# One encoder layer with a mixture of experts: the slot table's twelve scatters and its load go into GpSimd's overflow branch

## The reference, cut to what matters

```python
def _hier_moe(h, w_rg, b_rg, w_re, b_re, w_gate, w_up, w_down):
    ...
    grp_1h = jax.nn.one_hot(jnp.argmax(g_logits, -1), N_GROUPS, dtype=jnp.float32)
    ...
    top_v, top_i = lax.top_k(e_logits, TOP_K)
    top_w = jax.nn.softmax(top_v, axis=-1) * p_grp
    ...
    for e in range(N_EXPERTS):
        he = jax.nn.silu(t @ w_gate[e]) * (t @ w_up[e])
        y = y + comb[:, e:e + 1] * (he @ w_down[e])
```

## Time and profile before

| | |
|---|---|
| median of 3 runs | 1020.76 us (1020.22 to 1023.59) |
| profiled execution, span | 1024.1 us |
| TensorE busy | 910.2 us (89%) |
| GpSimd busy | 317.1 us (31%) |
| VectorE, ScalarE busy | 528.9 and 231.9 us |
| DMA moved | 165.11 MB, mean 161 GB/s |
| mean granted TensorE clock | 0.953 of 2.4 GHz |

### The profile page before, as it was taken

The page is one execution under the profiler, slowest core; times in us unless marked ns, Lnnn a source line. Parts: engine busy times, 40 slices in busy tenths (PEclk is TensorE's granted clock), DMA queues, the critical chain, the costliest instruction groups (busy, mean ns, idle before and its releaser), DMA issues.

```text
span 1024.1 us, 10105 instructions
## 1 busy us (share of the span) xinstructions
PE 910.2 (89%) x3322; PEld 470.7 (46%) x3322; DVE 528.9 (52%) x830; ACT 231.9 (23%) x578; POOL 317.1 (31%) x352
## 2 busy tenths in 40 slices
PE   4999999999979999999999999948969999999800
PEld 4555466444534444445567445544434444444300
DVE  4999999964533298736236554363311111111156
ACT  5321423333572112000014202131101111111101
POOL 6920043333454333300014313122342211122146
PEclk9999999999999999999999999967989999999955
DMA  9310300420020003120050314175998999998462
GB/s 340 137 42 0 124 0 22 143 61 22 1 95 30 1 0 122 43 83 1 0 205 1 121 44 164 62 307 224 417 378 318 417 422 418 389 413 346 165 256 116
DMA packets 46197, 165.11 MB, mean 161 GB/s; under 512 B 8640, under 2 KB 14144, under 8 KB 33856
## 3 DMA queue, kind: packets, MB, share of 16 engines
q1 hardware_dynamic: 39424, 151.85, 38.3%
q0 software_dynamic: 6720, 12.60, 3.3%
HBM read 156.88 MB, written 18.03 MB: 171 GB/s over the span
## 4 chain that ended last, share of the span: by engine, by line
PE 84%; POOL 4%; DVE 3%; ACT 3%; issue 3%; DMA 2%; POOLq 0%; DVEq 0%; ACTq 0%
PE ps L2009 17%; PE ps L2475 8%; PE ps L2504 7%; PE ps L2306 7%; PE ps L2171 6%; PE ps L2478 5%; PE ps L2241 5%; PE ps L2345 5%; PE ps L2279 5%; PE ps L2187 3%; PE ps L2137 2%; PE ps L2452 2%; PE ps L2112 2%; PE ps L2160 2%; PE ps L2148 2%
## 5 line engine op out<-in xcount | busy, mean ns | idle before, releaser
L1327 DVE SCALAR_TENSOR_TENSOR cat<-early,cpar,cat 128x798 f32<-128x798 f32 (+2 forms) x150 | 143.7, 958 | 4.9
L846 POOL TENSOR_SCALAR hT<-hT,rinv 128x512 f32<-128x512 f32 (+1 forms) x48 | 67.9, 1426 | 93.2 <-DVE rinv L1449 93.2
L2009 PE MATMUL ps<-ring,hT 128*128 128x512 f32 (+1 forms) x256 | 91.7, 519 | 0.0
L2009 PE MATMUL ps<-hT,ring 128*128 128x256 f32 (+1 forms) x256 | 84.7, 493 | 4.1 <-issue 2.5
L912 POOL DMA_INDIRECT pair_rows<-hT,sidx x22 | 22.1, 1005 | 182.0 <-DVE hT L1936 181.1
L1926 DVE COPY memx<-ps 128x256 f32<-128x256 f32 x22 | 9.3, 424 | 131.2 <-PE ps L2487 131.2
L2009 PEld LDWEIGHTS ps<-ring,hT 128*128 128x128 f32 x256 | 48.9, 193 | 39.6 <-issue 37.2
L2009 PEld LDWEIGHTS ps<-hT,ring 128*128 128x128 f32 x256 | 49.5, 194 | 38.0 <-issue 32.5
L853 POOL TENSOR_SCALAR memx<-memx,rinv 128x256 f32<-128x256 f32 x24 | 22.1, 927 | 129.6 <-DVE rinv L1405 129.6
L720 POOL TENSOR_SCALAR lnt<-mv 128x1 f32<-128x1 f32 x28 | 14.2, 508 | 154.6 <-DVE mv L748 153.4
L2504 PE MATMUL ps<-ring,memx 128*64 128x512 f32 (+1 forms) x144 | 58.8, 602 | 0.7 <-DVE memx L1926 0.7
(11 more groups left out here) (337 smaller groups left out, 1748.4 us busy)
## 6 DMA issues: line engine op xcount, KB each, us to landing
ring<-w_down SPq DMA_DIRECT2D x16, 1024.0 KB, 16.6
early<-w_gate SPq DMA_DIRECT2D x12, 1024.0 KB, 9.4
early<-w_up SPq DMA_DIRECT2D x12, 1024.0 KB, 13.4
ring<-w_gate SPq DMA_DIRECT2D x10, 1024.0 KB, 12.4
ring<-w_up SPq DMA_DIRECT2D x10, 1024.0 KB, 16.0
scr<-w_down SPq DMA_DIRECT2D x8, 1024.0 KB, 15.4
cat<-w_down SPq DMA_DIRECT2D x8, 1024.0 KB, 15.3
scr<-w_gate SPq DMA_DIRECT2D x5, 1024.0 KB, 9.2
```

The lines of the kernel that those rows point to most:

```text
L846: g.tensor_scalar(sprob[u % 4][:, 0:width], sprob[u % 4][:, 0:width], rinv[:, u % 4:u % 4 + 1], None, ALU.mult).then_inc(prob_ready, 1)
L1327: ins = v.scalar_tensor_tensor(out=out, in0=src, scalar=cpar[:, c, k:k + 1], in1=out, op0=ALU.mult, op1=ALU.add)
L2009: last = t.matmul(out_of(bank), lhs(k), rhs(k), start=(k == 0), stop=(k == KC - 1))
```

## The change

The twelve table scatters leave the loop of m = 2 and go to the start of GpSimd's branch for `n_over > 0`. The table's load leaves SyncE and is issued by GpSimd in the same branch, behind the wait for the scatters; the wait for the load stands there too. If `n_over` is zero, none of this is run. Nothing else differs.

```diff
--- before.py
+++ after.py
@@ -668,9 +668,6 @@
                     load_d(n % D_SLOTS, expert(n))
             sp.wait_ge(ctl_ready, 1)
             load_gb(3)
-            sp.wait_ge(table_done, 16 * 2 * NT)
-            sp.dma_start(tab[:, 0:BLOCKS * NE * 2].rearrange("p (b c) -> p b c", b=BLOCKS),
-                         table_dram.rearrange("(b p e) t -> p b (e t)", p=P, b=BLOCKS)).then_inc(tab_in, 16)
             n_over = sp.value_load(ctl[0:1, 0:1], min_val=0, max_val=LIST)
             with sp.Fori(0, LIST // 2) as i:
                 with sp.If(2 * i < n_over):
@@ -948,21 +945,23 @@
                     gather(m + 2)
                 if m >= 1:
                     scatter(m - 1)
-                if m == 2:
-                    pool.wait_ge(table_init, 16)
-                    for k in range(2):
-                        pool.wait_ge(slots_ready, k + 1)
-                        for i in range(NT):
-                            g.indirect_dma_start(table_dram, bass.IndirectOffsetOnAxis(ap=slots[:, k, i:i + 1], axis=0),
-                                                 tvals[:, i, k, :], None, bounds_check=T * NE - 1,
-                                                 oob_is_err=False).then_inc(table_done, 16)
             scatter(NSB - 1)
             pool.wait_ge(ctl_ready, 1)
-            pool.wait_ge(tab_in, 16)
             for b in range(2):
                 pool.wait_ge(rows_out[b], 16 * (NSB // 2))
             n_over = pool.value_load(ctl[0:1, 0:1], min_val=0, max_val=LIST)
             with pool.If(n_over > 0):
+                pool.wait_ge(table_init, 16)
+                for k in range(2):
+                    pool.wait_ge(slots_ready, k + 1)
+                    for i in range(NT):
+                        g.indirect_dma_start(table_dram, bass.IndirectOffsetOnAxis(ap=slots[:, k, i:i + 1], axis=0),
+                                             tvals[:, i, k, :], None, bounds_check=T * NE - 1,
+                                             oob_is_err=False).then_inc(table_done, 16)
+                pool.wait_ge(table_done, 16 * 2 * NT)
+                g.dma_start(tab[:, 0:BLOCKS * NE * 2].rearrange("p (b c) -> p b c", b=BLOCKS),
+                            table_dram.rearrange("(b p e) t -> p b (e t)", p=P, b=BLOCKS)).then_inc(tab_in, 16)
+                pool.wait_ge(tab_in, 16)
                 with pool.Fori(0, LIST // 2) as i:
                     with pool.If(2 * i < n_over):
                         cs = [pool.value_load(ctl[0:1, bass.ds(1 + LIST + 2 * i + b, 1)], min_val=0,
```

## The result

The changed kernel takes 1017.5 us in the median of 20 runs (1015.57 to 1024.77), the kernel before 1023.29 in 20 runs (1019.61 to 1029.38). The ratio is 0.9948 with a 95% interval of 0.9931 to 0.9966: faster by 5.3 us, 3.5 to 7.1. I had forecast 7.9 and, from the 3 runs then known, 1012.9 with a range up to 1017.0. So the direction was right, and the time is 0.5 us outside the range.

The account below looks back on a forecast made before the run. TensorE and the weight stream were taken as two near limits. Landing 7.5 + 0.4 = 7.9 us earlier at down(11), end 0: span 1024.1 to 1016.2, less 3.3 for the runs' median, 1012.9 us; range 1009.0 to 1017.0.

Parts of the forecast that it names:

- The burst holds gather(5) up: On GpSimd, twelve table scatters take 15.6 us before gather(5); without them it issues near 736.5 and TensorE's 8.33 us wait goes.
- TensorE's lead: How much earlier TensorE runs after down(3): 10.05 us gained less 1.5 us of waiting, 8.5 us (7.0 to 9.5).
- the wait at down(3): TensorE waits 0.5 to 3.0 us, taken as 1.5, for weights delayed by row transfers that move ahead.
- The weights set the start of down(11): At down(11) the weight load's landing, 7.9 us earlier (7.0 to 8.6), decides the start, not TensorE.
- the filled gap: The half-empty weight stream from 764 to 778 us fills, moving the landing for down(11) forward by 7.5 us.
- the first rival: The weight stream keeps some 3 us of its gap or loses speed to earlier row transfers: gain 5, 1015.8 us; 10%.
- The wait grows from 1.8 to some 2.2, and the gain from there is 7.9 us: At down(11) TensorE arrives at 847.7 and the weights at 849.9, so the kernel gains 7.9 us.
- the sign that I gave: Sign of being right: TensorE waits 1 to 4 us for weights at down(11).
- the stall at T(5): TensorE's 8.33 us wait for gather(5) before T(5), plus 1.7 us of work behind it at the 1.2 GHz clock.
- After down(11) nothing is given back: After down(11) every load waits on a buffer TensorE frees, so both move together and the gain stays.
- The end costs nothing: After the last scatter, the removed table load frees no time and the branch over a longer body costs 0 us.
- the jump: Rival: the branch over the longer overflow body costs an instruction fetch, 0 to 4.3 us, middle 2.2, giving 1015.1; 9%.

Follow-up runs that it names:

- b_spread: The kernel before, with the twelve table scatters issued one per turn, m = 2 to 13, instead of all in m = 2: ratio to before 0.9971, stage 260.1 us.
- a_warm18: The changed kernel with 18 unused 128x128 products on TensorE ahead of down(11): ratio to the kernel before 0.9928, stage 257.3 us.
- b_swap2: The kernel before with gate and up loads of experts 21 and 30 moved behind down matrices of 17, 18 and 26, 27: ratio 0.9996, stage 263.4 us.
- a_swap2: The changed kernel with gate and up loads of experts 21 and 30 moved behind down matrices of 17, 18 and 26, 27: 1012.65 us, ratio to before 0.9902.
- a_warm: The changed kernel with 36 unused 128x128 products on TensorE ahead of down(11): ratio to the kernel before 0.9972, stage 260.9 us.

## Why the prediction was right or wrong, point by point

- **The burst holds gather(5) up**: right. gather(5) was forecast at 736.5; it is at 737.42 in a trace whose stage starts 0.86 later. T(5) waits for nothing. b_spread shows that it is the burst.
- **TensorE's lead**: forecast 8.5 (7.0 to 9.5), measured 9.5, as T(6) to gu(10) all start 8.62 us earlier in a stage that starts 0.86 later. I had put the wait at down(3) at 1.5 us, and it is 0.36.
- **The weights set the start of down(11)**: right as a mechanism, with a size too large. The landing moved by 150.9 - 144.1 = 6.8 us, where I took 7.9 (7.0 to 8.6). By b_spread the table scatters are 0.7 of it (I took 0.4), if in a burst they cost what they cost spread out, which leaves 6.1 for the filled gap (I took 7.5). The gap did fill: the share is 0.99 or more in every 4 us from 760 to 780, so the first rival's gain of 5 us, near the one measured, would have come out right for a wrong reason. (A thinner stretch comes later, 291 GB/s at a share of 0.73 from 870 to 880, behind the wait at down(11); no product waits there.) What I put at nothing are bytes that come ahead of expert 17's. From the end of gu(0) nearly to the landing, 706 to 857 in the trace before, the DMA view has
```profile
DMA packets 10374, 58.12 MB, mean 385 GB/s; under 512 B 2278, under 2 KB 2278, under 8 KB 4293
```
and 707 to 851 in the changed kernel's
```profile
DMA packets 10181, 58.87 MB, mean 409 GB/s; under 512 B 1970, under 2 KB 1970, under 8 KB 4029
```
The 58.12 MB would take 142.1 us at 409 GB/s, 8.9 less than the 151 before, but 0.75 MB more are moved by then, and they take 1.8. Which transfers these are I didn't test.
- **"The wait grows from 1.8 to some 2.2, and the gain from there is 7.9 us"**: this is the step that failed. The wait grew to 4.49, since the lead was larger (9.5 for 8.5) and the landing later (6.8 for 7.9) than I took them; the sign that I gave, a wait of 1 to 4 us, is missed too. And down(11) then ran at the 1.2 GHz level, 5.9 us for 3.65, a term of 2.3 us that is nowhere in the sum. The row for it was there: I had counted 1.7 us for just that behind the stall at T(5), and didn't ask what a new wait would cost in the same way. 6.8 - 2.3 = 4.5 is the stage's gain: of the 3.4 us that it lacks, 2.3 are the clock and 1.1 the landing. a_warm18 takes the 2.3 back alone. Whether the wait of 2.2 us that I forecast would have cost anything is open: behind 1.80 down(11) took 3.65, and no run has a wait for weights between 1.80 and 3.79.
- **After down(11) nothing is given back**: right. All later blocks start 3.68 us earlier in the changed kernel's trace, to the end of down(21).
- **The end costs nothing**: right. From the last scatter's landing to the row loads it is 0.88 us now, 0.87 before; the chain, start, us, what:
```profile
968.95 2.59 DMA pair_rows<-hT,sidx
...
972.42 5.25 DMA cat<-pair_rows
```
The rule of the Trainium skill ("Runtime: NRT & Kernel Launch", instruction fetch mechanics), that a taken branch to a target outside the instruction pages held has to fetch it first, cost nothing here: the step took 0.88 us with the longer body and 0.87 with the shorter one. Whether the target lay outside in either, no run shows.
- **The time**: the other part of the miss is the base. I took the median of three runs, 1020.76; over 20 runs it is 1023.29. The gain forecast, from that base, would have given 1015.4. Taken as a gain, my range was 3.8 to 11.8 us, and the 5.3 measured lie in it, but by luck: I had made it that wide for a gap left in the stream and for the jump, neither of which occurred, and not for the clock.

## What to carry to other kernels

When a stall goes, follow the new slack to the next wait, and price that wait as a whole: what it adds, and the clock that TensorE loses behind it. Near a second limit the order of a saturated queue decides what a removed stall is worth: here 4.5 us in the old order of the loads and 9 to 10 in one that puts the loads with little slack first. An order edit may pay nothing by itself (b_swap2) and much together with another change (a_swap2).

## What the runs showed of the hardware that I had not expected

TensorE's granted clock was at 0.50 behind waits of 3.79 and 4.49 us in the middle of a stage with hardly any other idle time, while behind one of 1.80 us a block still took 3.65 us. With 18 unused products in such a wait it stayed at 1.00:
```profile
846.00:850.00 4.00, 3.65 (x18) 1.27 (x17) 0.00 (x0) 0.00 (x0) 0.00 (x0) 1.00 0.99 412
```
A plain fp32 product of 128x128 took 0.22 us in a_warm (8 us for 36), twice the 0.11 of a transpose of that size (eight in 0.9 us).
